# Gated-DeltaNet chunk inverses taken in pairs, the first chunk of each pair in reversed token order

## The chip, the cores and the metric

The kernel runs on one core of a Trainium2 chip. The metric is device time in microseconds (us). In profile rows PE is TensorE (its matmuls; PEld is its weight loads), DVE is VectorE, ACT is ScalarE, POOL is GpSimd and SP is SyncE.

## The reference

One step of a two-layer decoder trunk (float32, width 1024) for a prompt of 512 tokens and a sample group of 8 sequences of 4 tokens; all 544 tokens go through the same weights. Layer 0 mixes tokens with an HGRN2 recurrence, layer 1 with a gated DeltaNet; each is followed by a squared-ReLU MLP. The part that matters here is the inside of the second mixer, 8 heads of 128 by 128:

```python
G = jnp.cumsum(g, axis=-1)
decay = jnp.where(incl, jnp.exp(jnp.where(incl, diff, 0.0)), 0.0)
kk = jnp.einsum('nbhtk,nbhsk->nbhts', k, k)
M = jnp.eye(C, dtype=F32) + jnp.where(strict, beta[..., :, None] * kk * decay, 0.0)
u = lax.linalg.triangular_solve(M, v * beta[..., None], left_side=True, lower=True)
w = lax.linalg.triangular_solve(M, k * (beta * jnp.exp(G))[..., None], left_side=True, lower=True)
...
v_new = uc - jnp.einsum('bhtk,bhkv->bhtv', wc, S)
o = jnp.einsum('bhtk,bhkv->bhtv', qc, S) + jnp.einsum('bhts,bhsv->bhtv', ac, v_new)
S = glc[..., None, None] * S + jnp.einsum('bhsk,bhsv->bhkv', kc, v_new)
```

The kernel uses chunks of 128 tokens, so each head has four prompt chunks, and it needs the inverse of four unit lower triangular 128 by 128 matrices M.

## The kernel before

Everything is kept feature-major: a tile has 128 features as partitions and the 544 tokens along the row. The projections are float32 products made of three fp32r products (high by high, high by low, low by high); their matmuls all have one line, L411, and they come in steps of 6 (`tiles`, one of 8 slices of the contraction). Four units of 48 of them make one head's q, k, v and gate.

Each engine has its own program, and the order within an engine is as written; semaphores (`Steps`) join them. In the second mixer a loop runs over the heads. Its body on TensorE is `gdn_rec`, on ScalarE and VectorE `gdn_head`. While a head's recurrence runs, the three engines also prepare the next head: `gdn_prepare(slot, nxt)` is called between the steps, with the slots L0 to L6 beside the inverse and C0 to C2 beside the state update. TensorE fills its waits with projections for the coming heads: `more(2)` after the first product of a level and `more(1)` after the second (12 and 6 matmuls of L411), `later(1)` to `later(3)` in the state update. In the head before the last (head 6) `later` is empty, and in the last one (head 7) `more` is empty; there `later` does the output projection.

The inverse is built by doubling. At level m (2, 4, 8, 16, 32, 64) blocks of m by m are known on the diagonal. A level is a chain over the engines:

- **x**: for each of the four chunks, TensorE multiplies with the chunk's strict triangle `NL` (128 by 128, loaded as weights) the half of the columns of the transposed inverse `Tm` that this level needs: 64 columns (L667). ScalarE copies the result to `X` (L1173).
- **dt**: again for each chunk, `Tt` as weights and 64 columns of `X` (L700). VectorE writes the blocks that count into `Tm` with a predicated copy (L1763; step `pred{m}`).
- **tr**: TensorE transposes the four chunks of `Tm` (L449), ScalarE copies them to `Tt` (L1192; step `tt{m}`), and the next level's x waits for that.

At m = 64 the second product (L741) gives 64 rows of output and is followed by a plain copy (L1754, `pred64`), then the four chunks' state update goes one after the other: ks (L752), r (L1797), vn (L755), a ScalarE copy (L1208), dS (L758), S (L1424), with the outputs L759 and L761. Small sample products (L670, L685, L690, L692, L703, L735) run between. The last products of a head are `dSs0` (L767) and `dSs1` (L773); VectorE adds each to the sample states (L1811) and then ends the preparation of the next head.

In the head's preparation, L1614 is the silu product of k, q and v, L1694 puts the first level into `Tt`, L1682 and L1699 apply the triangle masks, L1214 copies the output. GpSimd does nothing but fill a tile with ones at the start.

Of the kernel before, what the change touches and what calls it, by code (L numbers as in the profile page):

```python
# [44 lines left out]
C_EYE, C_INCL, C_NSTR, C_IND, C_RESET, C_SEQ, C_INCLS, C_NSTRS, C_HSEL = 0, 128, 256, 384, 640, 1184, 1192, 1224, 1256  # L45
# [14 lines left out]
RS, VNS = T // 2, T // 2 + P  # L60


def shape_constants():
# [19 lines left out]
    for n, m in enumerate(LEVELS):  # L83
# [5 lines left out]
        cu[:, 1, n] = hit & (rh[:, None] == 1)  # L89
# [28 lines left out]
def build(nc, x_prompt, x_sample, state_hgrn, state_gdn, state_conv, norm_mix, norm_mlp, norm_final, hgrn_w_in,  # L118
          hgrn_lb, hgrn_out_norm, hgrn_w_out, gdn_w_in, gdn_conv_w, gdn_A_log, gdn_dt_bias, gdn_out_norm, gdn_w_out,
          mlp_w_up, mlp_w_down, const_f, const_u, y_prompt, y_sample, hgrn_p, hgrn_s, gdn_p, gdn_s, conv_p, conv_s):  # L120
    with ExitStack() as ctx:
# [3 lines left out]
        def sem(name):  # L125
            return ctx.enter_context(nc.semaphore(name))
# [52 lines left out]
        QL = hg["QL"].rearrange("p (a n) -> p a n", a=2)  # L179
        gd_vbig = [gd[n][0:TS, 0:4 * P] for n in ("Tm", "spare")]  # L180
# [42 lines left out]
        def levels(lists):  # L223
# [12 lines left out]
            gp=["x", "neg", "ls", "g", "g2", "scan", "dl"],  # L236
# [38 lines left out]
        )  # L275
        dt_ready = sem("dt_bias_ready")
# [27 lines left out]
        def blocks(ap, m):  # L304
            return ap.rearrange("p (n m) -> p n m", m=m)

# [84 lines left out]
        @block.gpsimd  # L391
        def _(pool):
            nc.gpsimd.memset(ones[:], 1.0).then_inc(ones_set, 1)


        @block.tensor
        def _(pe):
# [173 lines left out]
            def gdn_pre():  # L571
                v, s, t = st["gp"]
                pe.wait_ge(v.sem, v.after("dl", 0))
# [12 lines left out]
            def gdn_prepare(slot, h):  # L586
# [10 lines left out]
                if slot in ("L3", "L4"):  # L597
# [3 lines left out]
                    for b in range(2):  # L601
                        last = mm(rr[:, 2 + b, 0:HALF], cf[:, C_IND + g * P:C_IND + (g + 1) * P],
                                  work[:, b * HALF:(b + 1) * HALF], start=True, stop=True)
# [44 lines left out]
            def gdn_rec(h, prev, nxt, more, later):  # L648
# [7 lines left out]
                for n, m in enumerate(LEVELS[1:]):  # L656
# [31 lines left out]
                    if m == 64:  # L688
                        pe.wait_ge(s.sem, s.after("vns", h))
                        mm(rr[:, 1, 0:TS], X[0:TS, VNS:VNS + P], A[0:TS, TP:T], start=True, stop=False)  # L690
# [8 lines left out]
                    for c in range(NC):  # L699
                        last = mm(rr[:, 0, 256 + c * 64:256 + (c + 1) * 64], Tt[:, c * P:(c + 1) * P],  # L700
                                  X[:, c * 64:(c + 1) * 64], start=True, stop=True)
# [1223 lines left out]
```

## Time and profile before

| | |
|---|---|
| median of 3 runs | 1917.88 us (1913.43 to 1923.1) |
| time of the profiled execution | 1921.42 us |
| its span | 1919.6 us |
| mean granted TensorE clock | 0.94 |
| PE, PEld, DVE, ACT busy | 94%, 89%, 57%, 36% |
| POOL busy | 0.4 us, 5 instructions |

The profiled execution's time is 1.8 us more than its span. Stretches of the span: the first mixer ends near 400 us, the first MLP near 860 us, the second mixer near 1461 us, and then come output projection, second MLP and the last norm. The heads of the second mixer can be told by L773: its pairs start at 996.2, 1062.3, 1128.8, 1195.2, 1260.3, 1326.7, 1392.9 and 1460.7 us. In rows of a timeline a group's time reaches from its first start to its last end; matmuls overlap, so a group takes less of the engine than that. A float32 matmul is two MATMUL records in the trace (a transpose is one), so that four products are x8.

### The profile page before, as it was taken

Reading aid. Unit: us, or ns where it says so; the run is one execution under the profiler, and the core shown is the slowest. Engines: PE = TensorE matmul, PEld = TensorE weight load, DVE = VectorE, ACT = ScalarE, POOL = GpSimd, SP = SyncE. Lnnn points to the kernel's source line nnn. Section 1 sums busy time; section 2 is a strip of 40 time slices with the busy share of each in tenths; the row PEclk is TensorE's granted clock in tenths of the full one; section 3 lists DMA queues with packets and bytes.
Section 4 is the critical chain, followed back from the end, with each engine's and each line's share of the span. In section 5 each row is a group of like instructions: output and inputs, shape, how many; then the busy total and the mean of one; then the engine's idle time right before and its main releaser. Section 6 shows DMA issues by size and latency. Waiting matters only on the chain. (4 is left out here: it accounts for less than half of the span.)

```text
span 1919.6 us, 33969 instructions
## 1 busy us (share of the span) xinstructions
PE 1795.0 (94%) x13227; PEld 1699.2 (89%) x13227; DVE 1089.1 (57%) x1960; ACT 689.8 (36%) x1150; POOL 0.4 (0%) x5
## 2 busy tenths in 40 slices
PE   6999999989999999987899999999888999999997
PEld 5989999879999898986888888888768999999996
DVE  5777887755444343564567667766724543434344
ACT  5555555422222121223345445544512222222222
POOL 0000000000000000000000000000000000000000
PEclk9989999979999999997899999999758999999997
DMA  5222222213333232331121221122101323333321
GB/s 165 64 70 76 75 78 67 68 58 89 88 88 88 75 88 72 88 79 34 46 58 26 67 58 42 38 58 60 32 24 46 89 88 89 88 88 87 88 76 47
DMA packets 257436, 134.54 MB, mean 70 GB/s; under 512 B 6698, under 2 KB 256004, under 8 KB 257348
## 3 DMA queue, kind: packets, MB, share of 16 engines
q1 hardware_dynamic: 219488, 112.49, 20.6%
q10 hardware_dynamic: 37860, 20.76, 3.8%
q8 instruction: 69, 1.13, 0.2%
q14 instruction: 19, 0.16, 0.0%
HBM read 121.24 MB, written 12.00 MB: 69 GB/s over the span
## 5 line engine op out<-in xcount | busy, mean ns | idle before, releaser
L411 PE MATMUL pj<-xh,w_hi 128*128 128x272 f32 x2064 | 462.2, 306 | 22.2 <-DVE w_lo L1336 9.8
L867 ACT ACTIVATE w_hi<-w_raw 128x1024 fp32r<-128x1024 f32 x209 | 220.7, 1056 | 627.5 <-PE pj L411 624.9
L411 PE MATMUL pj<-xh,w_lo 128*128 128x272 f32 x2064 | 435.7, 293 | 0.0
L411 PE MATMUL pj<-xl,w_hi 128*128 128x272 f32 x2064 | 434.5, 293 | 0.0
L411 PEld LDWEIGHTS pj<-xh,w_hi 128*128 128x128 f32 x2064 | 330.8, 193 | 47.5 <-issue 25.8
L411 PEld LDWEIGHTS pj<-xl,w_hi 128*128 128x128 f32 x2064 | 332.7, 193 | 0.0
L411 PEld LDWEIGHTS pj<-xh,w_lo 128*128 128x128 f32 x2064 | 331.5, 194 | 0.0
L411 PE MATMUL pj<-oh,w_hi 128*128 128x272 f32 x1280 | 269.0, 292 | 14.3 <-DVE ol L1392 7.0
L1336 DVE TENSOR_TENSOR w_lo<-w_raw,w_hi 128x1024 fp32r<-128x1024 f32 x209 | 254.9, 1220 | 44.8 <-ACT w_hi L867 44.8
L411 PE MATMUL pj<-oh,w_lo 128*128 128x272 f32 x1280 | 266.8, 290 | 0.0
L411 PE MATMUL pj<-ol,w_hi 128*128 128x272 f32 x1280 | 265.9, 289 | 0.0
L411 PEld LDWEIGHTS pj<-oh,w_hi 128*128 128x128 f32 x1280 | 203.1, 190 | 18.0 <-DVE ol L1392 7.9
L411 PEld LDWEIGHTS pj<-ol,w_hi 128*128 128x128 f32 x1280 | 203.2, 190 | 0.0
L411 PEld LDWEIGHTS pj<-oh,w_lo 128*128 128x128 f32 x1280 | 201.8, 191 | 0.0
L1832 DVE TENSOR_TENSOR ws<-pj,rstd 128x544 f32<-128x544 f32 x64 | 46.4, 725 | 198.9 <-PE pj L411 194.5
L1844 DVE TENSOR_TENSOR xT<-xT,pj 128x544 f32<-128x544 f32 x48 | 34.6, 721 | 167.9 <-PE pj L411 167.9
L449 PE MATMUL rr<-cf,ws 128*128 128x128 f32 (+2 forms) x440 | 73.2, 305 | 13.3 <-ACT ws L1273 4.8
L449 PEld LDWEIGHTS rr<-cf,ws 128*128 128x128 f32 (+2 forms) x440 | 53.6, 153 | 25.2 <-issue 10.4
L667 PEld LDWEIGHTS rr<-ws 128*128 128x128 f32 x384 | 52.0, 208 | 21.6 <-ACT ws L1192 16.7
L1372 DVE TENSOR_TENSOR xT<-xT,pj 128x544 f32<-128x544 f32 x32 | 23.1, 721 | 81.9 <-PE pj L411 81.9
L667 PE MATMUL rr<-ws 128*128 128x64 f32 x384 | 56.9, 295 | 10.1 <-ACT ws L1192 7.8
L509 PEld LDWEIGHTS rr<-ws 128*128 128x128 f32 x448 | 59.5, 204 | 5.0 <-DVE ws L1494 3.5
(278 smaller groups left out, 2040.8 us busy)
## 6 DMA issues: line engine op xcount, KB each, us to landing
w_raw<-in_mlp_w_up_dram SPq DMA_DIRECT2D x64, 512.0 KB, 3.9
w_raw<-in_mlp_w_down_dram SPq DMA_DIRECT2D x64, 512.0 KB, 3.7
w_raw<-in_hgrn_w_in_dram SPq DMA_DIRECT2D x32, 512.0 KB, 4.0
w_raw<-in_gdn_w_in_dram SPq DMA_DIRECT2D x32, 512.0 KB, 4.2
out_dram<-S ACTq DMA_DIRECT2D x16, 512.0 KB, 3.5
S<-in_state_hgrn_dram ACTq DMA_DIRECT2D x8, 512.0 KB, 4.0
w_raw<-in_hgrn_w_out_dram SPq DMA_DIRECT2D x8, 512.0 KB, 3.6
S<-in_state_gdn_dram ACTq DMA_DIRECT2D x8, 512.0 KB, 4.0
```

Source lines behind the costliest of these rows:

```text
L411: last = mm(pj[:, s, b, 0:HALF], w[:, s, k, :], v[:, k, b * HALF:(b + 1) * HALF], start=(k == 0 and a == 0), stop=(k == KT - 1 and a == 2))
L449: return nc.tensor.transpose(out, in_, cf[0:n, C_EYE:C_EYE + n])
L509: last = mm(rr[:, n % 2, c * 64:(c + 1) * 64], KL[:, n % 2, c * P:(c + 1) * P], QL[:, n % 2, c * 64:(c + 1) * 64], start=True, stop=True)
L667: last = mm(rr[:, 0, c * 64:(c + 1) * 64], NL[:, cols], first_half(Tm[:, cols], m), start=True, stop=True)
L867: f(w_hi[:, c % SPLIT], w_raw[:, slot], ACT.Copy).then_inc(w_high, 1)
L1336: tt(w_lo[:, c % SPLIT], w_raw[:, c % RAW], w_hi[:, c % SPLIT], ALU.subtract).then_inc(w_low, 1)
L1372: tt(halves(xT[:, k]), halves(xT[:, k]), computed(U, r, k), ALU.add).then_inc(unit_out, 1)
L1832: tt(halves(B[:, k % 2]), computed(U, r, k), halves(rstd[:]), ALU.mult).then_inc(unit_out, 1)
L1844: tt(halves(xT[:, k]), halves(xT[:, k]), computed(U, g * (2 * KT), KT + k), ALU.add).then_inc(unit_out, 1)
```

## The change

The first chunk of each of the two pairs (chunks 0 and 2) is kept in reversed token order in everything that the chunk's matrices are made of. A matrix that was upper triangular becomes lower triangular by that, and so the columns that one chunk's inverse needs at a level and the rows that the other one needs lie in complementary halves. From level 4 on, one 128 by 128 weight tile holds the needed half of both chunks' `NL` (called `NLm`, put together by GpSimd in two copies a level), one holds the needed half of both chunks' `Tt` (`Ttm`, put together by ScalarE in two copies), and one product with 128 columns replaces two with 64. The transposes and level 2 stay as they were. The parts:

- TensorE: x at levels 4 to 64, dt at 4 to 32 and the product of level 64 are 2 products with 128 columns in place of 4 with 64. x of a level waits for GpSimd too.
- ScalarE: `tt2` to `tt16` are two copies of 128 elements in place of one of 512; the output copy is two of 256, one of them reversed; some copies before the first head are split in three.
- VectorE: each `pred` is two instructions of half the size, `pred64` too; silu of q, k and v is two of 256 in place of one of 512; the mask products keep their size; one step (`turn`, three copies) is new before the first head.
- GpSimd: 10 copies a head, 128 elements a partition each.
- Two products that spread a row over the partitions read 32 rows of `ones` and `work` in place of 128.

```diff
+        NLm = [gd["spare"][:, a * 2 * P:(a + 1) * 2 * P] for a in range(2)]
+        Ttm = gd["X"][:, TTM:TTM + 2 * P]
...
+        def pair_half(ap, m, odd, half):
+
+            return over_pairs(ap)[:, :, odd * P:(odd + 1) * P].rearrange("p q (n two m) -> p q n two m", two=2, m=m)[:, :, :, half, :]
...
+        def interleaved(ap, m, odd):
+
+            return ap.rearrange("p (q n two m) -> p q n two m", q=2, two=2, m=m)[:, :, :, odd]
+
+        def earlier(ap, q, m):
+
+            return bass.AP(ap.tensor, ap.offset + q * 2 * P + m, [ap.ap[0], [P - m, 2], [2 * m, P // (2 * m)], [1, m]])
...
+            def mix(h):
+
+                va, t = st["ga"][0], st["gr"][2]
+                for n, m in enumerate(LEVELS[2:], 1):
+                    waits = []
+                    if m == 4:
+                        waits.append((va.sem, fixed(pool, va.after("nl", h))))
+                        if not isinstance(h, int):
+                            waits.append((t.sem, fixed(pool, t.after("dSs1", h - 1))))
+                    if m >= 16:
+                        waits.append((t.sem, fixed(pool, t.after(f"x{m // 4}", h))))
...
+                    for odd in range(2):
+                        last = nc.gpsimd.tensor_copy(interleaved(NLm[n % 2], m, odd), pair_half(gd["NL"][:, 0:TP], m, odd, odd))
+                    mixed.did(last, f"m{m}")
...
-                    for c in range(NC):
-                        cols = slice(c * P, (c + 1) * P)
-                        last = mm(rr[:, 0, c * 64:(c + 1) * 64], NL[:, cols], first_half(Tm[:, cols], m),
-                                  start=True, stop=True)
...
+                        pe.wait_ge(mixed.sem, mixed.after(f"m{m}", h))
+                        for q in range(NC // 2):
+                            last = mm(rr[:, 0, q * P:(q + 1) * P], NLm[n % 2][:, q * P:(q + 1) * P], earlier(Tm, q, m),
+                                      start=True, stop=True)
...
+                        for q in range(NC // 2):
+                            last = mm(rr[:, 0, 256 + q * P:256 + (q + 1) * P], Ttm[:, q * P:(q + 1) * P],
+                                      X[:, q * P:(q + 1) * P], start=True, stop=True)
...
-                for c in range(NC):
-                    last = mm(rr[0:m, 0, 256 + c * m:256 + (c + 1) * m], X[:, c * m:(c + 1) * m],
-                              Tt[:, c * P + m:(c + 1) * P], start=True, stop=True)
+                for q in range(NC // 2):
+                    last = mm(rr[:, 0, 256 + q * P:256 + (q + 1) * P], X[:, q * P:(q + 1) * P], later_ends(Tt, q),
+                              start=True, stop=True)
...
-                    last = f(Tt[:, 0:TP], rr[:, 1, :], ACT.Copy)
+                    if m < LEVELS[-2]:
+                        for odd in range(2):
+                            last = f(interleaved(Ttm, 2 * m, odd), pair_half(rr[:, 1, :], 2 * m, odd, odd), ACT.Copy)
+                    else:
+                        last = f(Tt[:, 0:TP], rr[:, 1, :], ACT.Copy)
...
-                s.did(f(oo[:, 0:TP], rr[:, 1, :], ACT.Copy), "oo")
+                f(blocks(oo[:, 0:TP], P)[:, 0::2, ::-1], blocks(rr[:, 1, :], P)[:, 0::2, :], ACT.Copy)
+                s.did(f(blocks(oo[:, 0:TP], P)[:, 1::2, :], blocks(rr[:, 1, :], P)[:, 1::2, :], ACT.Copy), "oo")
...
-                    tt(dst[:, 0:TP], pr[:, row, 0:TP], ng[:, row, 0:TP], ALU.mult)
+                    for (o, a), (_, b) in list(zip(by_position(dst, pr[:, row, 0:T]), by_position(dst, ng[:, row, 0:T])))[0:2]:
+                        tt(o, a, b, ALU.mult)
...
-                    last = pred(first_half(Tm[:, 0:TP], m), blocks(mask[:, 1, n, 0:TP // 2], m), blocks(rr[:, 0, 256:512], m))
+                    for odd in range(2):
+                        last = pred(pair_half(Tm[:, 0:TP], m, odd, 1 - odd), pair_cols(mask[:, 1, n, 0:TP // 2], m, odd),
+                                    pair_cols(rr[:, 0, 256:512], m, odd))
```

TensorE's program in the last head, before, from x of level 4 to x of level 32 (one row is a group of equal matmuls; L667 is x, L700 dt, L449 a transpose, L685 the sample states):

```order
L667 MATMUL rr<-ws 128x64 x4
L700 MATMUL rr<-ws 128x64 x4
L449 MATMUL rr<-cf,ws 128x128 x8
L449 MATMUL rr<-cf,ws 32x128
L667 MATMUL rr<-ws 128x64 x4
L685 MATMUL rr<-ws,S 128x4 x8
L700 MATMUL rr<-ws 128x64 x4
L449 MATMUL rr<-cf,ws 128x128 x4
L667 MATMUL rr<-ws 128x64 x4
L700 MATMUL rr<-ws 128x64 x4
```

And the same place after (L726 is x, L764 dt, L502 a transpose, L744 the sample states):

```order
L726 MATMUL rr<-ws 128x128 x2
L764 MATMUL rr<-ws 128x128 x2
L502 MATMUL rr<-cf,ws 128x128 x8
L502 MATMUL rr<-cf,ws 32x128
L726 MATMUL rr<-ws 128x128 x2
L744 MATMUL rr<-ws,S 128x4 x8
L764 MATMUL rr<-ws 128x128 x2
L502 MATMUL rr<-cf,ws 128x128 x4
L726 MATMUL rr<-ws 128x128 x2
L764 MATMUL rr<-ws 128x128 x2
```

Only the number and the width of the x and dt products differ; nothing changes its place.

VectorE's program in the loop over the heads, before, up to `pred8` (L1606 and L1427 are the next head's convolution, L1749 a small sample step, L1763 the predicated copy):

```order
L1606 SCALAR_TENSOR_TENSOR pr<-xp,hcw,pr 128x568
L1293 REGISTER_ALU
L1427 SCALAR_TENSOR_TENSOR ng<-pr 128x568
L1293 REGISTER_ALU
L1749 TENSOR_TENSOR rt<-rr,eGs 128x32
L115 REGISTER_ALU
L1763 COPY_PREDICATED ws<-cu,rr 128x32x8
```

And after (L1687 and L1505 are the convolution, L1835 the sample step, L1852 the predicated copy):

```order
L1687 SCALAR_TENSOR_TENSOR pr<-xp,hcw,pr 128x568
L1371 REGISTER_ALU
L1505 SCALAR_TENSOR_TENSOR ng<-pr 128x568
L1371 REGISTER_ALU
L1835 TENSOR_TENSOR rt<-rr,eGs 128x32
L116 REGISTER_ALU
L1852 COPY_PREDICATED ws<-cu,rr 128x2x8x8 x2
```

Nothing moved here either: the predicated copy has become two, at the same place behind the next head's convolution.

## Rows read from the trace of the kernel before

**Rows 1.** The page, its first two parts: span and busy time

```profile
span 1919.6 us, 33969 instructions
PE 1795.0 (94%) x13227; PEld 1699.2 (89%) x13227; DVE 1089.1 (57%) x1960; ACT 689.8 (36%) x1150; POOL 0.4 (0%) x5
```

**Rows 2.** Busy by stretch: length, PE, PEld, DVE, ACT, POOL, PEclk, DMA share, GB/s

```profile
1195.00:1260.00 65.00, 60.87 (x451) 54.01 (x450) 45.20 (x102) 31.89 (x70) 0.00 (x0) 1.00 0.19 51
1260.00:1326.00 66.00, 61.91 (x449) 55.05 (x447) 44.91 (x102) 31.96 (x70) 0.00 (x0) 0.97 0.18 50
1278.50:1289.70 11.20, 11.06 (x88) 10.43 (x88) 10.67 (x19) 5.46 (x13) 0.00 (x0) 1.00 0.14 41
1291.00:1298.00 7.00, 6.12 (x45) 5.39 (x44) 5.09 (x12) 6.92 (x16) 0.00 (x0) 1.00 0.13 31
1396.00:1447.40 51.40, 43.74 (x187) 38.91 (x188) 12.46 (x34) 8.71 (x21) 0.00 (x0) 0.50 0.08 22
```

**Rows 3.** PE timeline: the last product (`dSs1`) of heads 3, 4 and 5

```profile
1195.17 0.67 PE L773 MATMUL rr<-ws,kdTs 32*128 32x512 f32 x1
1260.30 0.67 PE L773 MATMUL rr<-ws,kdTs 32*128 32x512 f32 x1
1326.70 0.67 PE L773 MATMUL rr<-ws,kdTs 32*128 32x512 f32 x1
```

**Rows 4.** PE timeline of head 5: start, time, line, count, idle before

```profile
1266.25 0.49 PE L411 MATMUL pj<-xh,w_hi 128*128 128x272 f32 x2 [0.48 <-DVE xp L1597]
1271.45 1.10 PE L667 MATMUL rr<-ws 128*128 128x64 f32 x8 [0.17 <-ACT ws L1194]
1275.64 1.10 PE L700 MATMUL rr<-ws 128*128 128x64 f32 x8 [1.10 <-ACT ws L1173]
1291.67 1.10 PE L667 MATMUL rr<-ws 128*128 128x64 f32 x8 [0.58 <-ACT ws L1192]
1311.44 0.38 PE L755 MATMUL rr<-ws 128*128 128x128 f32 x2
1313.26 1.06 PE L622 MATMUL rr<-ws 128*128 128x128 f32 x8
```

**Rows 5.** DVE timeline of head 5

```profile
1278.58 0.76 DVE L1738 TENSOR_TENSOR ws<-rr,gcols 128x256 f32<-128x256 f32 x2 [1.29 <-PE rr L449]
1280.98 2.50 DVE L1606 SCALAR_TENSOR_TENSOR pr<-xp,hcw,pr 128x568 f32<-128x568 f32 x3
1284.28 0.43 DVE L1763 COPY_PREDICATED ws<-cu,rr 128x256 f32<-128x256 uint8 x1
1289.83 0.45 DVE L1763 COPY_PREDICATED ws<-cu,rr 128x256 f32<-128x256 uint8 x1 [0.16 <-PE rr L700]
1303.10 0.69 DVE L1614 TENSOR_TENSOR ws<-pr,ng 128x512 f32<-128x512 f32 x1
1308.77 0.29 DVE L1421 COPY Sp<-rr 128x128 f32<-128x128 f32 x1 [0.75 <-PE rr L758]
```

**Rows 6.** ACT timeline of head 5

```profile
1291.02 0.60 ACT L1192 ACTIVATE ws<-rr 128x512 f32<-128x512 f32 x1 [2.20 <-PE rr L449]
1297.41 0.60 ACT L1192 ACTIVATE ws<-rr 128x512 f32<-128x512 f32 x1
1316.67 0.28 ACT L1208 ACTIVATE ws<-rr 128x128 f32<-128x128 f32 x1 [4.24 <-PE rr L755]
```

**Rows 7.** PE timeline of head 7

```profile
1424.89 1.97 PE L700 MATMUL rr<-ws 128*128 128x64 f32 x8 [0.47 <-ACT ws L1173]
1427.45 1.12 PE L449 MATMUL rr<-cf,ws 128*128 128x128 f32 x4 [0.59 <-DVE ws L1763]
1429.25 1.97 PE L667 MATMUL rr<-ws 128*128 128x64 f32 x8 [0.47 <-ACT ws L1192]
```

**Rows 8.** PE timeline ahead of the first head, and POOL's instructions

```profile
865.57 1.30 PE L449 MATMUL rr<-cf,gt 128*128 128x128 f32 x5 [10.72 <-ACT gt L1031]
L393 POOL MEMSET ones<- 128x128 f32 x1 | 0.2, 204 | 0.3 <-POOLq L1913 0.3
```

More of the change, by code:

```diff
@@ L393, in _ @@
             nc.gpsimd.memset(ones[:], 1.0).then_inc(ones_set, 1)
+            def mix(h):
[8 more added lines that the diff above has]
+                        waits.append((t.sem, fixed(pool, t.after(f"x{m // 4}", h))))
+                    pool.wait_ge(c_in, 16 * N_CONST)
+                    for sem_, value in waits:
+                        pool.wait_ge(sem_, value)
+                    for odd in range(2):
+                        last = nc.gpsimd.tensor_copy(interleaved(NLm[n % 2], m, odd), pair_half(gd["NL"][:, 0:TP], m, odd, odd))
+                    mixed.did(last, f"m{m}")
+            mix(0)
+            with pool.Fori(1, H) as h:
+                mix(h)
         @block.tensor
@@ L572, in gdn_pre @@
                 v, s, t = st["gp"]
-                pe.wait_ge(v.sem, v.after("dl", 0))
+                pe.wait_ge(v.sem, v.after("turn", 0))
                 pe.wait_ge(s.sem, s.after("eg", 0))
@@ L601, in gdn_prepare @@
                     for b in range(2):
-                        last = mm(rr[:, 2 + b, 0:HALF], cf[:, C_IND + g * P:C_IND + (g + 1) * P],
-                                  work[:, b * HALF:(b + 1) * HALF], start=True, stop=True)
+                        last = mm(rr[:, 2 + b, 0:HALF], ones[32 * g:32 * (g + 1), :],
+                                  work[32 * g:32 * (g + 1), b * HALF:(b + 1) * HALF], start=True, stop=True)
                     t.did(last, name)
@@ L664, in gdn_rec @@
                         pe.wait_ge(s.sem, s.after(f"tt{LEVELS[n]}", h))
-                    for c in range(NC):
-                        cols = slice(c * P, (c + 1) * P)
-                        last = mm(rr[:, 0, c * 64:(c + 1) * 64], NL[:, cols], first_half(Tm[:, cols], m),
-                                  start=True, stop=True)
+                    if n == 0:
+                        for c in range(NC):
+                            cols = slice(c * P, (c + 1) * P)
+                            half = Tm[:, cols].rearrange("p (n two m) -> p n two m", two=2, m=m)[:, :, 1 - c % 2, :]
+                            last = mm(rr[:, 0, c * 64:(c + 1) * 64], NL[:, cols], half, start=True, stop=True)
+                    else:
[3 more added lines that the diff above has]
+                                      start=True, stop=True)
                     if smp:
@@ L698, in gdn_rec @@
                     pe.wait_ge(s.sem, s.after(f"x{m}", h))
-                    for c in range(NC):
-                        last = mm(rr[:, 0, 256 + c * 64:256 + (c + 1) * 64], Tt[:, c * P:(c + 1) * P],
-                                  X[:, c * 64:(c + 1) * 64], start=True, stop=True)
+                    if n == 0:
+                        for c in range(NC):
+                            last = mm(rr[:, 0, 256 + c * 64:256 + (c + 1) * 64], Tt[:, c * P:(c + 1) * P],
+                                      X[:, c * 64:(c + 1) * 64], start=True, stop=True)
+                    else:
+                        for q in range(NC // 2):
+                            last = mm(rr[:, 0, 256 + q * P:256 + (q + 1) * P], Ttm[:, q * P:(q + 1) * P],
+                                      X[:, q * P:(q + 1) * P], start=True, stop=True)
                     if smp:
```

79 lines of the change are left out of this document (54 added, 25 removed).

## The prediction

> **What bounds the kernel now.** I read the page first [rows 1]: TensorE is busy for 94% of the span, VectorE for 57%. That looks like a kernel in which every matmul taken away counts. So the next view is the busy time by stretch in the second mixer [rows 2]. A head takes 65 to 66.5 us, TensorE is busy for about 61 of it and VectorE for 45. A busy share does not say who waits for whom, so I then read the timelines of the three engines in head 5, one of the five heads of the loop, in order of time. There TensorE waits seldom, but each wait is for a copy of ScalarE or a product of VectorE [rows 4], and two stretches have no slack on another engine: from 1278.58 to 1289.7 VectorE is busy for 10.67 of 11.20 us, and from 1291.0 to 1298.0 ScalarE for 6.92 of 7.00 us [rows 2]. In both, the step of the inverse that TensorE needs next (the predicated copies of levels 8 and 16, the copy `tt32`) is queued behind work for the next head [rows 5, 6]. TensorE's fill work just covers them. The loop heads are balanced: TensorE is as late as VectorE and ScalarE, not later.
>
> The last head is another case. There is no next head and no fill, its clock is 1.2 GHz (granted 0.50 over 51.4 us, rows 2), and TensorE waits only for the step that it has itself just released, 0.47 to 0.59 us each [rows 7]. There every matmul in the chain counts.
>
> **What one product costs.** Eight records with 128 columns (L622, four products) take 1.06 us and two (L755) take 0.38: (1.06 - 0.38) / 6 = 0.11 us a record at 2.4 GHz. Eight records with 64 columns (L667) take 1.10 us, as much as eight with 128 [rows 4]. So a product costs the same with twice the columns, and a group that falls from 8 records to 4 gives back 4 x 0.11 = 0.45 us. At 1.2 GHz the step is (1.97 - 1.12) / 4 = 0.21 us [rows 7], and a group gives back 0.85 us. Nine groups a head are of this kind (x of 4 to 64, dt of 4 to 32); the product of level 64 loads only 64 columns of weights before, and I take 0.2 us for it. That removes 9 x 0.45 + 0.2 = 4.25 us of TensorE's work from each of heads 0 to 6, and 9 x 0.85 + 0.25 = 7.9 us from head 7.
>
> **What the other engines get.** ScalarE: one copy of 512 elements is 0.60 us, one of 128 is 0.28 [rows 6]; if the second starts 0.1 us before the first ends, two take 0.46, so `tt2` to `tt16` come 0.14 us earlier. VectorE: a predicated copy of 256 elements is 0.43 to 0.45 us, a plain copy of 128 is 0.29 [rows 5]; two halves should be 0.48, 0.05 more. Silu is 0.69 for 512 elements [rows 5]; two halves are some 0.09 more, three times a head. The output copy grows by 0.1 us in front of transposes that have 12 matmuls of fill ahead of them: nothing. Reversed rows are not in the trace; bounds are nothing and a doubling of 0.35 us per half, and I take nothing, as VectorE's strided products of 256 elements are no slower.
>
> **A loop head, step by step** (head 5, its own times):
> - Level 4: x waits 0.17 us for `tt2` [rows 4] and starts 0.14 earlier; it is 0.45 shorter, but the transposes behind it wait for VectorE, so 0.35 is left. The wait of 1.10 us before dt is for ScalarE, which is busy for the next head behind those transposes: it stays. dt gives 0.45; VectorE, still in L1336, gives the predicated copy only part of it. When the key transposes are done, 0.55 us is gained.
> - From there VectorE has no gap (L1738 at 1278.58) until `pred16`, except the 0.16 us in front of it [rows 5]. x and dt of levels 8 and 16 are 1.8 us shorter, and all of this turns into waits of TensorE for `pred8` and `pred16`. Gained: 0.55 + 0.16 - 2 x 0.05 = 0.6.
> - `tt16` 0.14 earlier: x of level 32, which waits 0.58 us for it [rows 4], starts 0.75 earlier. Then ScalarE has no gap up to `tt32` at 1297.41 [rows 6], so x of level 64 is also 0.75 earlier, and the 0.9 us of x and dt of level 32 is lost.
> - x of level 64 gives 0.45: 1.2. Level 64's product, then silu and `pred64` in VectorE's gapless row take back 0.15, and silu of v about 0.05: **1.0 us a head** of 4.25.
>
> **The sum.** Heads 1 to 5: 5 x 1.0 = 5.0. Head 0 has no head before it to finish, so VectorE has three full rows less (about 0.7 us each, as silu); of the 1.8 us lost in that stretch I count half or so: 2.0. Head 6 has the same front and no projections behind: 1.2. Head 7: 7.9, plus two `tt` copies on the path 0.3, less the split copies 0.3: 7.9. Before the first head TensorE stands 10.72 us for a chain of small steps that ends in a 0.65 us exponential [rows 8]; the split copies and the new step put perhaps 0.2 on it, and silu in the first preparation 0.3: -0.5. GpSimd: 10 copies a head of 128 elements; the only row of its size is a fill, 0.204 us [rows 8]. Level 64's may start when x of level 16 is done, and from x of level 32 at 1291.67 [rows 4] to the end of `tt32` at 1298.0 [rows 6] alone are 6.3 us, so TensorE won't wait for them. What they cost is what they take from VectorE: nothing, or 8 of 10 copies at full length in heads 0 to 6, 56 x 0.2 = 11.4 us. No row shows the two together; I take 0.3 us a head, nearer to nothing as the copies are short against the convolution they meet (three in 2.50 us, rows 5): -2.1. Together 5.0 + 2.0 + 1.2 + 7.9 - 0.5 - 2.1 = **13.5 us**. The profiled execution's 1921.4 us would become 1907.9; that execution is 3.5 us above the median, and from the median 1917.9 I forecast **1904.4 us**.
>
> **The rivals.**
> - *TensorE bounds all heads after all*, since it is busy for 94%: then 7 x 4.25 + 7.9 - 0.5 = 37 us, 1881. Against it stand the two gapless stretches. Chance 0.1.
> - *GpSimd holds VectorE* (the case on the other side). Place: level 32's copies start behind x of level 8, in the middle of VectorE's gapless stretch, those of level 64 behind x of 16, those of 4 and 8 behind `dSs1`, where TensorE waits 0.48 us for VectorE [rows 4]. Without the GpSimd term the gain is 15.6 us. With 0.204 us for each of 56 copies it is 4.2 (1913.7); at 0.28 us a copy it is gone; from 0.45 us a copy the kernel is slower by more than 0.5%. At 0.5 us: 56 x 0.5 - 15.6 = 12.4 us slower, 1930. Chance of about no change by this 0.15, of slower 0.1. The Trainium skill bears on it: GPSIMD Engine Reference, section Key points, says that GpSimd shares its SBUF interfaces with VectorE and contends with instructions in a two-port mode or with two SBUF inputs. The convolution in that stretch has two SBUF inputs, so by this rule the sum would lie nearer to the 4.2 us; no row here shows it.
> - *The clock.* Head 4, at full clock throughout, takes 65.13 us and head 5, with granted 0.97, takes 66.40 [rows 2, 3]: one dip costs 1.27 us. TensorE will wait some 3 us more in each head. Two more dips in each of seven heads would cost 17.8 us: 1922. Against it: the added waits lie where TensorE has slack then, so a dip there costs less. Chance of ending near no change 0.12. The other way, the last head's stretch of 51.4 us at 1.2 GHz, with 43.7 us of TensorE in it, could get a higher clock as its waits get shorter against its work; half of that back would be about 11 us more, 1893. Chance 0.05. The Trainium skill (TensorE: Matmul & The Clock Gate, Part 1) says that the granted clock follows how busy TensorE has been of late; the last head's 0.50 agrees.
> - *The change doesn't do what it says*: if 128 columns cost twice 64, nothing would be gained. The row of L622 excludes it.
>
> **How the numbers follow.** Forecast 0.48, own range 1898 to 1911. A measurement of this kernel tells about 0.5%, 9.6 us, from no change, so faster means below 1908.3: most of the forecast (0.40), TensorE-bound 0.1 and the better clock 0.05 make 0.55; same 0.35; slower 0.10. Leaving out the TensorE-bound case (0.1) and the slower one (0.1) gives 1886 to 1919.
>
> **What the profile after would show.** In the loop heads: x and dt of levels 4 to 64 as x4 in 0.6 us; TensorE's waits grow by about 3 us a head, with new ones of some 1 us in front of the transposes of levels 8 and 16, for the predicated copy; the period of L773 falls by about 1 us; VectorE's stretch between kdT and `pred16` keeps its 11 us. In the last head: from dt of level 16 to x of level 32 it is 4.36 us before [rows 7] and should be about 3.4; all of its chain shrinks by 8. POOL: 80 copies. Wrong would be: L1606 longer than 0.83 us each (2.50 for three) where a POOL copy runs, POOL copies over 0.4 us, a period that falls by 4 us, or a granted clock in heads 1 to 5 below 0.95.

## The result

The changed kernel takes **1900.27 us** (median of 7 runs, 1897.56 to 1903.4) where the kernel before takes 1917.88 (7 runs); the ratio is 0.9907, with a 95% interval of 0.9896 to 0.9918. That is 17.6 us less; the forecast was 13.5 less (1904.4), with a stated range of 1898 to 1911. The profiled execution has a span of 1898.5 us against 1919.6, so 21.1 us less. Of these, 4.2 us lie ahead of the second mixer's first convolution step (at 889.15 us before, at 884.94 after), where nothing was changed; over the 14 profiled executions of this document that point lies between 878.6 and 889.1 us.

The page of the kernel after, its span and busy time, and the row of GpSimd's copies:

```profile
span 1898.5 us, 33650 instructions
PE 1762.5 (93%) x12907; PEld 1658.5 (87%) x12907; DVE 1095.6 (58%) x2043; ACT 684.4 (36%) x1194; POOL 43.2 (2%) x85
L441 POOL COPY ws<-ws 128x128 f32<-128x128 f32 x80 | 42.8, 568 | 1360.9 <-DVE ws L1766 914.1
```

Busy time by stretch after: head 4, head 5, VectorE's row from the key decay to `pred16` in head 5, and the last head; columns as in [rows 2]:

```profile
1183.00:1248.20 65.20, 59.25 (x413) 51.57 (x412) 46.10 (x111) 31.20 (x75) 5.26 (x10) 0.97 0.19 50
1248.20:1312.50 64.30, 57.84 (x412) 49.95 (x412) 46.09 (x111) 31.22 (x75) 5.26 (x10) 1.00 0.18 51
1266.20:1277.30 11.10, 9.92 (x75) 9.09 (x76) 10.71 (x20) 5.17 (x13) 2.83 (x4) 1.00 0.15 43
1378.10:1437.90 59.80, 50.68 (x250) 42.46 (x250) 17.21 (x49) 10.89 (x33) 4.47 (x10) 0.63 0.07 19
```

VectorE's row ahead of `pred16` is as long and as full as before (10.71 of 11.10 us; 10.67 of 11.20 in [rows 2]), while TensorE's busy time in it fell from 11.06 to 9.92. A head at full clock has 3.0 us less of TensorE's work than before (57.84 against 60.87, [rows 2]) and is 0.8 us shorter (64.33 against 65.13, [rows 3]).

TensorE's timeline of head 5 after, the places that [rows 4] shows of before and the new waits (L726 is x, L764 dt, L502 the transposes, L485 the feature sum):

```profile
1259.50 0.71 PE L726 MATMUL rr<-ws 128*128 128x128 f32 x4
1263.59 0.71 PE L764 MATMUL rr<-ws 128*128 128x128 f32 x4 [1.10 <-ACT ws L1246]
1272.58 0.66 PE L502 MATMUL rr<-cf,ws 128*128 128x128 f32 x4 [1.13 <-DVE ws L1852]
1277.88 0.66 PE L502 MATMUL rr<-cf,ws 128*128 128x128 f32 x4 [0.19 <-DVE ws L1852]
1279.15 0.71 PE L726 MATMUL rr<-ws 128*128 128x128 f32 x4 [0.50 <-ACT vTs L1277]
1294.52 1.18 PE L485 MATMUL rr<-ws,ones 128*128 128x272 f32 x4 [0.42 <-DVE ws L1705]
```

Eight records became four, and the group behind dt of level 4 starts 0.46 us after it (1263.59 to 1264.05) where it was 0.92 (1275.64 to 1276.56). The copy of x of level 4 is waited for as long as before (1.10 us). In front of the transposes of level 8 there is a new wait of 1.13 us for the predicated copy. VectorE in the same head, against [rows 5]:

```profile
1266.22 0.76 DVE L1824 TENSOR_TENSOR ws<-rr,gcols 128x256 f32<-128x256 f32 x2 [1.29 <-PE rr L502]
1272.04 0.49 DVE L1852 COPY_PREDICATED ws<-cu,rr 128x128 f32<-128x128 uint8 x2
1277.34 0.48 DVE L1852 COPY_PREDICATED ws<-cu,rr 128x128 f32<-128x128 uint8 x2
1278.66 0.74 DVE L1696 TENSOR_TENSOR ws<-pr,ng 128x256 f32<-128x256 f32 x2
```

And TensorE in the last head, against [rows 7]:

```profile
1404.45 1.22 PE L764 MATMUL rr<-ws 128*128 128x128 f32 x4 [0.47 <-ACT ws L1246]
1406.33 1.11 PE L502 MATMUL rr<-cf,ws 128*128 128x128 f32 x4 [0.65 <-DVE ws L1852]
1407.97 1.23 PE L726 MATMUL rr<-ws 128*128 128x128 f32 x4 [0.32 <-ACT ws L1267]
```

From dt of level 16 to x of level 32 it is 3.52 us where it was 4.36.

**A table for all that follows.** Length of the heads in the profiled executions, from one head's last product (`dSs1`) to the next head's. In brackets: how many short stretches of 3.4 us at 1.2 GHz begin in a loop head. A head without one has a granted clock of 1.00, with one 0.97, with two 0.95. A ratio is taken against runs of the kernel before that were made beside that kernel (medians 1916.1 for e1 to e4, 1919.8 for e5 to e7, 1917.7 for e8 to e11, 1917.4 for e12), so ratios compare better than medians do.

| kernel | median us | ratio (95%) | heads 1 to 5 | head 6 | head 7 |
|---|---|---|---|---|---|
| before | 1917.9 | 1 | 66.1 (1), 66.4 (1), 66.4 (1), 65.1 (0), 66.4 (1) | 66.2 | 67.8 |
| after | 1900.3 | 0.9907 (0.9896 to 0.9918) | 64.7 (2), 65.1 (1), 65.1 (1), 65.2 (1), 64.3 (0) | 65.5 | 59.9 |
| e1 | 1934.3 | 1.0091 (1.0075 to 1.0107) | 67.9 (2), 68.2 (2), 68.2 (2), 68.2 (2), 68.2 (2) | 66.6 | 62.3 |
| e2 | 1932.8 | 1.0091 (1.0076 to 1.0106) | 67.9 (2), 68.2 (2), 68.2 (2), 68.2 (2), 68.2 (2) | 66.4 | 69.3 |
| e3 | 1910.3 | 0.9966 (0.9952 to 0.998) | 64.7 (1), 65.0 (2), 65.1 (2), 65.1 (2), 65.1 (1) | 65.6 | 69.3 |
| e4 | 1902.9 | 0.9926 (0.9912 to 0.994) | 64.8 (2), 65.1 (1), 64.5 (0), 65.1 (2), 65.1 (1) | 64.9 | 59.9 |
| e5 | 1926.7 | 1.0041 (1.0026 to 1.0057) | 67.4 (1), 68.2 (2), 67.6 (1), 66.2 (0), 67.7 (1) | 64.1 | 68.9 |
| e6 | 1900.8 | 0.9908 (0.9892 to 0.9924) | 64.7 (1), 65.0 (1), 64.4 (0), 65.0 (1), 65.0 (1) | 65.8 | 59.9 |
| e7 | 1914.6 | 0.9983 (0.997 to 0.9995) | 66.1 (1), 65.2 (0), 65.1 (0), 65.1 (0), 66.4 (1) | 63.8 | 68.7 |
| e8 | 1934.5 | 1.0095 (1.0081 to 1.011) | 69.6 (3), 67.0 (1), 68.3 (2), 68.3 (2), 68.3 (2) | 66.4 | 67.4 |
| e9 | 1913.4 | 0.9975 (0.9964 to 0.9986) | 65.5 (1), 65.9 (1), 65.9 (1), 66.6 (2), 67.7 (3) | 64.0 | 62.0 |
| e10 | 1913.4 | 0.9975 (0.996 to 0.999) | 65.2 (1), 65.9 (1), 67.0 (2), 68.0 (3), 65.5 (1) | 62.5 | 59.9 |
| e11 | 1906.5 | 0.9947 (0.9932 to 0.9963) | 65.7 (2), 64.5 (1), 63.8 (0), 66.0 (2), 63.8 (0) | 65.3 | 61.8 |
| e12 | 1893.6 | 0.9873 (0.9852 to 0.9895) | 63.1 (0), 63.4 (0), 64.0 (1), 63.4 (0), 64.1 (1) | 62.6 | 62.2 |

### The profile page after: what moved, and what is told of

The parts are those of the page before. It is cut to its first block and busy times, and to the rows that moved or that the text cites. A ratio compares the mean times of both kernels' runs of the same rounds, so it can differ in the third digit from the quotient of the medians.

```text
span 1898.5 us, 33650 instructions
## 1 busy us (share of the span) xinstructions
PE 1762.5 (93%) x12907; PEld 1658.5 (87%) x12907; DVE 1095.6 (58%) x2043; ACT 684.4 (36%) x1194; POOL 43.2 (2%) x85
## 3 DMA queue, kind: packets, MB, share of 16 engines
q1 hardware_dynamic: 219488, 112.49, 21.1%
q8 instruction: 68, 1.11, 0.2%
## 5 line engine op out<-in xcount | busy, mean ns | idle before, releaser
L502 PE MATMUL rr<-cf,ws 128*128 128x128 f32 (+2 forms) x440 | 74.6, 310 | 20.8 <-DVE ws L1852 9.6
L502 PEld LDWEIGHTS rr<-cf,ws 128*128 128x128 f32 (+2 forms) x440 | 54.4, 154 | 36.8 <-DVE ws L1852 14.4
L441 POOL COPY ws<-ws 128x128 f32<-128x128 f32 x80 | 42.8, 568 | 1360.9 <-DVE ws L1766 914.1
L562 PEld LDWEIGHTS rr<-ws 128*128 128x128 f32 x448 | 58.7, 202 | 5.0 <-DVE ws L1572 3.5
```

The source lines that it names most:

```text
L441: last = nc.gpsimd.tensor_copy(interleaved(NLm[n % 2], m, odd), pair_half(gd["NL"][:, 0:TP], m, odd, odd))
L502: return nc.tensor.transpose(out, in_, cf[0:n, C_EYE:C_EYE + n])
L562: last = mm(rr[:, n % 2, c * 64:(c + 1) * 64], KL[:, n % 2, c * P:(c + 1) * P], QL[:, n % 2, c * 64:(c + 1) * 64], start=True, stop=True)
```

## The experiments

**e1, e2, e3: the pairs in the last head alone, nowhere, in the loop heads alone.** The token order and all that belongs to it stays; the products go chunk by chunk where `paired` is false:

```
+                    elif not paired:      # e1: nxt is None; e2: never; e3: nxt is not None
+                        for c in range(NC):
+                            cols = slice(c * P, (c + 1) * P)
+                            half = Tm[:, cols].rearrange("p (n two m) -> p n two m", two=2, m=m)[:, :, 1 - c % 2, :]
+                            last = mm(rr[:, 0, c * 64:(c + 1) * 64], NL[:, cols], half, start=True, stop=True)
+                    else:
```

(dt and the `tt` copy likewise; GpSimd mixes only for paired heads.)

> The new token order stays in all heads; the products of x (levels 4 to 64) and dt (levels 4 to 32) are paired only in head 7, heads 0 to 6 take eight records again, with one tt copy each and no GpSimd copies. Theory (loop heads are bound by VectorE and ScalarE, the last head by TensorE): the last head gives 7.9 us, the order itself costs about 2, so 1912 us against 1917.9 before. Rival (the loop heads give nothing, what the changed kernel gained there is the clock's doing): the same 17.6 us as the fully changed kernel, about 1900.

> Token order, split predicated copies, split silu and the merged dt of level 64 stay; no other product is paired, one tt copy a level, GpSimd copies nothing. Theory: overhead alone, 0.5 us ahead of the first head, about 0.25 a loop head (silu 0.09 three times, predicated copies 0.05 each in a gapless row of VectorE), less 0.4 for level 64's dt in the last head: 2 us slower, 1920. Rival (reversed rows or split instructions cost more than the forecast, and the pairs gain more than it): 5 us slower or more, 1923 and up. Rival (order is free): 1918.

> Pairs in heads 0 to 6 only, with their GpSimd copies; head 7 takes eight records. Theory: all of the gain but the last head's 7.9 us, so about 9.7 us faster, 1908; heads 0 to 6 then gave 11 to 12 us over the order alone, 1.3 to 1.6 each. Rival (loop heads give nothing): 1918 to 1920.

The order without pairs is 16.7 us slower than before (1932.8 against 1916.1), not 2, and e1, expected at 1912, takes 1934.3; e3 came at 1910.3 where 1908 was expected. The pairs in the loop heads then give 22.5 us (e3 against e2), 3.1 us a head in the traces; those in the last head give 10.0 us in the medians (after against e3; 11.3 by the ratios) and 9.4 in the traces. e1 and e2 have the same ratio although e1's last head is 7.0 us shorter in its trace. In e1's profiled execution 3.9 us more than in e2's lie ahead of the first convolution step and 4.9 behind the last head, with a wait of 2.79 us for weights of the second MLP that the other traces don't have; where the timed runs lose the 7 us was not seen.

Where did the order's 17 us come from? Head 5 of e2 in pieces, the 1.2 GHz stretches apart:

```profile
1261.30:1282.50 21.20, 19.32 (x144) 16.87 (x143) 12.35 (x38) 8.02 (x23) 0.00 (x0) 1.00 0.36 104
1282.80:1286.20 3.40, 3.40 (x19) 3.40 (x17) 2.52 (x5) 1.44 (x4) 0.00 (x0) 0.52 0.00 0
1286.50:1306.40 19.90, 18.97 (x136) 16.42 (x136) 15.10 (x34) 11.55 (x25) 0.00 (x0) 1.00 0.09 26
1306.70:1310.10 3.40, 3.40 (x18) 3.11 (x17) 3.35 (x8) 1.98 (x4) 0.00 (x0) 0.52 0.00 0
1310.50:1329.50 19.00, 17.71 (x132) 15.76 (x130) 11.57 (x28) 8.54 (x17) 0.00 (x0) 1.00 0.11 30
```

Two short stretches at half clock, and all five heads of e2 have them at the same two places, 21 and 45 us behind `dSs1`. Before, one head has one or none. In e2 both places lie at the end of a group of 8 products of 4 columns (16 records; the expectations call them 16 products): from 0.2 us before the end of its last record to 1.0 us behind it, and 0.2 to 1.7 us behind it in the kernel before. That these groups let the clock fall was a theory to test.

**e5, e6, e7: those groups widened**, in the order-only kernel, after and before.

```
-    last = mm(rr[:, 1, b * SLEN:(b + 1) * SLEN], S0[:, b, :], K[:, TP + b * SLEN:TP + (b + 1) * SLEN], start=True, stop=True)
+    last = mm(rr[:, 1, b * SLEN:TS], S0[:, b, :], K[:, TP + b * SLEN:T], start=True, stop=True)
```

(the products with `qe` likewise; those add up, so in these three kernels the sample rows of the output differ)

> The order-only kernel (e2) with one more edit: the two groups of 16 products with 4 columns a head (sample states, named sks and os) take all columns up to the end of the sample block, 32 down to 4; those of os then add wrong values in the sample rows, so the output differs there. Theory formed after e1 to e4: the order itself costs nothing; its 17 us are TensorE's clock. In the traces each half-clock stretch of 3.4 us in heads 1 to 5 begins 0.4 to 2 us behind one of these two groups; the order-only kernel has two in each head (68.2 us), the one before has one (66.4) or none (65.1). If the groups are what lets the clock fall, the stretches go, the heads take 65.1 us, and the kernel about 1910 (23 us less than e2's 1933). Rival (split and reversed instructions are what costs 17 us): heads stay at 68 us, 1933. Rival (something else lets the clock fall): the stretches stay where they are.

> The changed kernel with the same widening of the sks and os products (sample rows differ). Its heads take 65.1 us with one or with two half-clock stretches and 64.3 to 64.5 with none. Theory: the stretches go from the heads, 0.7 us each for six heads, some 4 us less: 1896. Rival (the last head also gets a higher clock): up to 10 us less, 1890. Rival (no effect on the clock): 1900.

> The kernel before with the same widening (sample rows differ). Theory: heads at 65.1 us throughout where most take 66.4, so 5 to 8 us less: 1908 to 1912; at an equal clock the changed kernel's heads are then 0.7 us shorter, which is the value of the pairs in a loop head without the clock. Rival (no effect on the clock): 1916.

The theory holds in part. e5 has 5 short stretches in heads 1 to 5 instead of 10 and gives back 6 us in the medians (9.6 by the ratios), of 23; e7 has 2 instead of 4, and its ratio is 0.9983; e6 changes nothing in the time. Expected were 1910, 1896 and 1908 to 1912; the medians are 1926.7, 1900.8 and 1914.6. Some of the stretches that are left begin elsewhere (34 us behind `dSs1` in e5). What lets the clock fall is therefore not settled. But these runs give heads at full clock in three kernels, to be compared without the clock. The first row is e7 (the work of before), the second e5 (the order alone), the third e6 (the work of after):

```profile
1186.60:1251.70 65.10, 61.01 (x452) 54.15 (x452) 45.34 (x101) 31.91 (x70) 0.00 (x0) 1.00 0.19 51
```

```profile
1193.90:1260.10 66.20, 61.50 (x448) 54.02 (x448) 45.77 (x111) 31.96 (x71) 0.00 (x0) 1.00 0.18 50
```

```profile
1118.80:1183.20 64.40, 57.91 (x413) 50.04 (x412) 46.13 (x111) 31.21 (x75) 5.26 (x10) 1.00 0.19 51
```

From `dSs1` to `dSs1` the order costs 1.05 us a head (66.18 against 65.13) and the pairs give 1.85 (to after's 64.33; e6's own head is 64.37): **0.80 us a head net**, where the prediction had 1.0. Set side by side step by step, e5 loses 0.23 us up to the end of the broadcast `gb` (0.09 in front of it, 0.14 in it), 0.34 at `bb`, some 0.2 at predicated copies, and 0.25 late in the head, in VectorE's row: `pred64` in two copies (0.51 us from first start to the next instruction, 0.34 before) and silu in two halves (0.67 against 0.60).

**e8: the broadcast alone, in the kernel before.** The change also altered the products that spread a head's gate and beta over all rows. The prediction had passed over this edit.

```
-    last = mm(rr[:, 2 + b, 0:HALF], cf[:, C_IND + g * P:C_IND + (g + 1) * P],
-              work[:, b * HALF:(b + 1) * HALF], start=True, stop=True)
+    last = mm(rr[:, 2 + b, 0:HALF], ones[32 * g:32 * (g + 1), :],
+              work[32 * g:32 * (g + 1), b * HALF:(b + 1) * HALF], start=True, stop=True)
```

> The kernel before with one edit of the change alone: the broadcasts gb and bb take 32 rows of ones and of the gates in place of 128 rows of an indicator (L602). At full clock in both, the two groups and what stands behind them took 0.23 and 0.43 us more in the order-only kernel than in the one before. Theory (those two groups of four products are 0.6 us of the 1.1 us by which a loop head got longer through the new order): heads at full clock 65.13 to 65.6 or 65.7 us, some 3 to 5 us in all, unless the clock's stretches fall otherwise: 1920 to 1922 against 1917. Rival (the order of the tokens, the split instructions, cost it all): 65.13 stays.

e8's heads 2 and 3, with one and with two short stretches:

```profile
1062.60:1129.60 67.00, 62.88 (x453) 55.40 (x452) 45.18 (x101) 31.98 (x70) 0.00 (x0) 0.97 0.18 49
1129.60:1197.90 68.30, 64.20 (x453) 56.92 (x452) 45.18 (x101) 32.08 (x70) 0.00 (x0) 0.95 0.18 48
```

With one short stretch the head takes 66.98 us where it takes 66.41 before: 0.57 us for this edit, as expected. Group by group, against before's head 5, whose stretch lies at the same place: 0.23 us up to the end of `gb`, 0.34 at `bb`, nothing behind. TensorE in e8's head 2, the second group (`bb`) and what follows it, and the same place in head 5 of before:

```profile
1095.29 1.18 PE L602 MATMUL rr<-ws,ones 32*128 32x272 f32 x4
1096.40 0.52 PE L411 MATMUL pj<-xh,w_hi 128*128 128x272 f32 x2
```

```profile
1292.62 1.14 PE L602 MATMUL rr<-ws,cf 128*128 128x272 f32 x4
1293.39 0.61 PE L411 MATMUL pj<-xh,w_hi 128*128 128x272 f32 x2
```

The same four records with 32 rows in place of 128 hold the next group back by 1.11 us, not 0.77. But the median rose by 16.8 us, and the expectation of 3 to 5 was wrong: 0.57 us in seven heads are 4. Most of the rest goes with the clock. In the traces heads 1 to 5 are 10.9 us longer than before: 2.9 are the edit, and the other 8 go with six more short stretches (10 against 4), 1.3 us each. In the timed runs the mean granted clock has a median of 0.935 in e8 against 0.943 before; over 68 runs of the kernel before, 0.001 of clock goes with 1.4 us (a line fitted through them), so 0.008 is 11 us by this estimate. The line holds for one kernel only: e5 takes 12 us more than e7 at the same mean clock (0.945). e2 (0.938) and e8 have the same pattern, a head of 68.2 to 68.3 us with two short stretches each at the same places.

**e4: three times the GpSimd copies.**

```
+    for again in ("a", "b", ""):     # each level's two copies three times, each behind the one before
         for odd in range(2):
             last = nc.gpsimd.tensor_copy(interleaved(NLm[n % 2], m, odd), pair_half(gd["NL"][:, 0:TP], m, odd, odd))
```

> The changed kernel with every GpSimd copy made three times over (30 a head instead of 10, 160 more in all, the same values to the same place). Theory (where GpSimd meets VectorE, GpSimd's copy is what gets longer, 0.29 to 0.9 us, and VectorE's convolution keeps its 0.81 us a step): no change, 1900 within 2 us, though POOL is busy for some 130 us. Rival (GpSimd takes its own time from VectorE, 0.2 us a copy, 140 more copies in heads 0 to 6): 28 us slower if all count, 10 to 15 if those in the gapless stretches do: 1910 or more.

POOL is busy for 112.9 us instead of 43.2, and the time is 1902.9 where 1898 to 1902 was expected. The ratio is 0.9926 (0.9912 to 0.994) against the changed kernel's 0.9907 (0.9896 to 0.9918): the intervals just overlap, so a small cost, 3.6 us by the ratios for 160 more copies, is not excluded, but the 28 us of the rival are, and so are its 10 to 15. A head at full clock by busy time, and VectorE's convolution in the groups of instructions:

```profile
1121.60:1186.10 64.50, 57.85 (x412) 49.95 (x412) 46.42 (x111) 31.20 (x75) 14.17 (x30) 1.00 0.19 51
```

```profile
L1692 DVE SCALAR_TENSOR_TENSOR pr<-xp,hcw,pr 128x568 f32<-128x568 f32 x72 | 58.4, 811 | 6.2 <-ACT pr L1124 4.5
```

Twenty more copies a head cost VectorE 0.3 us of busy time (46.42 against 46.09), its convolution 2 ns a step (811 against 809). A head at full clock is 0.2 us longer (64.51 against 64.33). What gets longer is GpSimd's copy: two of them take 1.67 us beside the loop head's convolution and 0.53 us in the last head, where VectorE is mostly idle (POOL's timeline after):

```profile
1337.89 1.67 POOL L441 COPY ws<-ws 128x128 f32<-128x128 f32 x2 [6.17 <-PE rr L726]
1404.11 0.53 POOL L441 COPY ws<-ws 128x128 f32<-128x128 f32 x2 [4.36 <-PE rr L726]
```

**e9, e10, e11: which engine sets a loop head.** Steps of VectorE, in e11 of ScalarE too, are moved in the changed kernel: e9 puts `pred8` ahead of the third tap of k's convolution, e10 also puts the third tap of q behind `pred16`, e11 also puts the z unit's weight split behind the copy of x of level 4 (ScalarE) and behind `pred4` (VectorE).

```
     for j in taps:
+        if j == 3 and between is not None:
+            between()                                  # e9: sr1 and pred8
...
-    convolve("q", "qtap", 1, Q_ROW)                    # in L3
+    convolve("q", "qtap", 1, Q_ROW, (1, 2))            # e10: in L3
+    convolve("q", "qtap", 1, Q_ROW, (3,))              # e10: in L4, behind pred16
...
     s.did(last, f"x{m}")
+    if nxt is not None and m == 4:
+        high(nxt * 4, U_GIN + 3)                       # e11: no longer in L1
```

> The changed kernel with the predicated copies of level 8 moved on VectorE ahead of the third tap of k's convolution; nothing else. TensorE's wait in front of the transposes of level 8 (1.13 us in head 5) goes. Theory of the prediction (VectorE has no gap from the key decay to pred16, so it sets when level 16 goes on): the wait in front of level 16's transposes grows from 0.19 to about 1.2 us, the period stays at 65.1 (one half-clock stretch) and the kernel at 1900. Rival (TensorE sets the time of the stretch): 1.1 us a head in seven heads, 1892 to 1893.

> As e9, and the third tap and the minimum of q's convolution (1.6 us of VectorE) moved behind pred16. Theory: VectorE's gapless row ahead of pred16 is 1.6 us shorter, so what e9 could not give comes: 0.8 to 1.2 us a head, period 64 us, 1893 to 1895. Rival (ScalarE's gapless row up to tt32 or the later silu takes it back): 1899 to 1901. Rival (TensorE-bound, e9 gave it already): the same as e9.

> As e10, and the weight split of the z unit put behind the copy of x of level 4 on ScalarE and behind pred4 on VectorE, where TensorE waits 1.10 us for that copy (head 5) in both kernels. Theory: another 0.5 to 1 us a head, 1888 to 1890. Rival (the unit's weights then come late for TensorE's fill, or VectorE's row behind is pushed by 1.2 us): as e10 or up to 5 us slower.

Expected were 1900, 1893 to 1895 and 1888 to 1890; the medians are 1913.4, 1913.4 and 1906.5. e9 loses 0.8 us a head at one short stretch (65.9 against 65.1), and its kernel 13 us: some 6 are those 0.8 us in seven heads, its last head is 2.1 us longer, and two of its heads have two and three short stretches. The timelines of VectorE, ScalarE and TensorE in e9's head 2:

```profile
1082.41 0.49 DVE L1841 COPY_PREDICATED ws<-cu,rr 128x128 f32<-128x128 uint8 x2 [0.31 <-PE rr L764]
1085.85 0.75 DVE L1509 SCALAR_TENSOR_TENSOR ng<-pr,ng 128x568 f32<-128x568 f32 x1 [0.49 <-ACT ng L1126]
```

```profile
1084.43 0.68 ACT L1124 ACTIVATE ng<-ng 128x568 f32<-128x568 f32 x1 [0.56 <-DVE ng L1505]
1085.72 0.43 ACT L1267 ACTIVATE ws<-rr 128x128 f32<-128x128 f32 x2
```

```profile
1086.28 0.71 PE L726 MATMUL rr<-ws 128*128 128x128 f32 x4 [1.55 <-ACT ws L1267]
1090.25 0.66 PE L502 MATMUL rr<-cf,ws 128*128 128x128 f32 x4 [0.56 <-DVE ws L1868]
```

The wait in front of the transposes is gone, and TensorE stands 1.55 us one step later: the copy `tt8` is queued on ScalarE behind exp and log of k, which need the convolution that is now later. VectorE's row got two gaps, 0.31 and 0.49 us, and `pred16` came 0.77 us later. So it is not TensorE that sets this stretch (taking its wait away gave nothing, as it came back one step later), and a gap in VectorE's row costs its full length, as the prediction had it; but ScalarE stands right behind VectorE, which it had not. e10 shows the same 1.56 us wait for `tt8` and no gain over e9. e11 alone brings something: its wait in front of dt of level 4 fell from 1.10 to 0.15 us, and its heads at full clock take 63.8 us, 0.5 less than after's 64.3; yet its median is 6 us above the changed kernel's, with two short stretches in heads 1 and 4 and a last head of 61.8 us.

**e12: 128 rows again, and the x4 copy first.** The broadcast reads one indicator column for all 128 columns; of e11 only the z unit's weight split is kept.

```
-    last = mm(rr[:, 2 + b, 0:HALF], ones[32 * g:32 * (g + 1), :],
-              work[32 * g:32 * (g + 1), b * HALF:(b + 1) * HALF], start=True, stop=True)
+    last = mm(rr[:, 2 + b, 0:HALF], cf[:, C_ROW[g]:C_ROW[g] + 1].broadcast_to([P, P]),
+              work[:, b * HALF:(b + 1) * HALF], start=True, stop=True)
```

> The changed kernel with two edits: the broadcasts gb and bb take 128 rows again (an indicator column that is read for all 128 columns), and the weight split of the z unit stands behind the copy of x of level 4 on ScalarE and behind pred4 on VectorE. Theory: gb and what follows gets 0.14 us shorter and bb 0.34, the wait of 1.10 us in front of dt of level 4 goes; a loop head at full clock takes 63.6 to 64.0 us where the changed kernel takes 64.33, 3 to 6 us in all: 1895. Rival (VectorE's and ScalarE's gapless rows take back the 128-row part): 63.8, as e11. Rival (a new rhythm brings more half-clock stretches, as in e9 to e11): 1900 to 1906, with heads at full clock no longer than 64.

Head 4 of e12 by busy time, and dt of level 4 (its wait was 1.10 us) and the broadcast `bb` in TensorE's timeline there:

```profile
1175.60:1239.00 63.40, 57.17 (x413) 50.02 (x412) 46.01 (x111) 31.21 (x75) 4.79 (x10) 1.00 0.19 52
```

```profile
1190.05 0.71 PE L766 MATMUL rr<-ws 128*128 128x128 f32 x4 [0.16 <-ACT ws L1249]
1206.12 1.08 PE L657 MATMUL rr<-ws,cf 128*128 128x272 f32 x4
```

This is the fastest kernel, 1893.6 us, ratio 0.9873, and its interval (0.9852 to 0.9895) lies below the changed kernel's. A head at full clock takes 63.4 us, 0.9 less than after and 0.4 less than e11, and three of five heads are at full clock. Its two edits were not made one by one, so how the 0.9 us divide between them is open.

## Why the prediction was right, point by point

- **The time.** 17.6 us against 13.5 forecast, inside the stated range. By the profiled executions: heads 1 to 5 gave 6.1 us (330.5 to 324.4; forecast 5.0), of which 4.0 are the five heads at full clock and 2.1 come from short stretches that cost less after than before, head 6 0.65 (1.2), head 7 7.87 (7.9), and the stretch from the first convolution step to the end of head 0 3.9 (1.5), with a granted clock of 0.90 against 0.87 there, which carries part of it. GpSimd took little (forecast 2.1): by e4, whose 20 more copies lengthen a full-clock head by 0.2 us, 10 copies are 0.1 us a head, an estimate. Together 18.5; 4.2 lie ahead of the change, and 1.6 were lost behind it, where TensorE is at half clock for 31.5 us in place of 27.1. That the sum fits within 4 us is partly luck: the loop heads at full clock gave less than forecast, and the clock and the stretch before head 1 more.
- **The price of a product** held: x and dt of eight records became four, and the group behind starts 0.41 to 0.46 us sooner (forecast 0.45). By busy time it is less: a group's row falls from 1.10 to 0.71 us, and a head has 3.6 us less (e5 against e6), not 4.25; TensorE's idle time in a head at full clock grew by 2.3 us, not 3. And e2 against e1, both at half clock through the inverse, is 7.0 us for the last head (forecast 7.9 net).
- **Head by head.** At full clock the gain is 0.80 us, not 1.0. Along the head (after's head 5 against e7's head at 1186.6): key transposes 0.32 us earlier (forecast 0.55), transposes behind `pred16` 0.39 (0.6), x of level 32 0.43 (0.75), x of level 64 0.59 (0.75), dt of level 64 1.13 (1.2), end 0.80 (1.0). The shape is right: little until `pred16`, next to nothing between there and x of level 64, most from level 64. The 1.2 us that TensorE has gained by the end of level 8's dt are down to 0.1 at the transposes behind it, in a new wait of 1.13 us, as forecast; the one at level 16 is 0.19 instead of about 1.
- **The step that was missed** is an edit without a term: the broadcast with 32 rows, which the sum put at nothing without a reason. It costs 0.57 us a head in the kernel before. In the changed kernel it lies partly in time that TensorE would wait anyhow; there it was only taken out together with e11's move.
- **VectorE sets the loop heads**: half right. The gapless row stayed (10.71 of 11.10 us), and e9 shows that a gap in it is paid in full. But e9 and e10 show ScalarE as late as VectorE at `tt8`, which the prediction named only for `tt32`.
- **Small terms**: two `tt` copies 0.45 us (0.46), predicated copies 0.48 to 0.50 (0.48), silu 0.07 more (0.09), the wait before the first head 10.90 after 10.72 (0.2 more), reversed rows nothing that shows: right.
- **The GpSimd rival** is out by e4 with its price of 0.2 us a copy. One sign that the prediction named for it did appear, POOL copies over 0.4 us: the 80 copies take 0.57 us in the mean and 1.72 at the longest. None of the others did: the convolution kept 0.81 us a step, the period fell by 0.8 us at full clock and not by 4, and heads 1 to 5 together have a granted clock of 0.97. So the length of a copy says nothing here of what it costs. By the Trainium skill (GPSIMD Engine Reference, section Key points) GpSimd contends with VectorE's instructions that have two SBUF inputs, as the convolution has; the trace agrees that they meet (0.53 us for two copies alone, 1.67 beside it), but here VectorE's convolution kept 809 ns a step, and GpSimd's copy paid.
- **The last head** has the right sum by luck: 7.0 us are the pairs, 2.4 come from a higher clock (e1 to after: 3.3 us at granted 0.94 in the middle, rows below, and an earlier return to full clock; a small part of the 11 us of the prediction's better-clock case), and 1.6 go the other way (e2's last head is longer than that of before, 69.3 against 67.8, by more time at half clock).

  The middle of the last head after, and the same place in e1:

```profile
1398.50:1401.80 3.30, 2.54 (x20) 2.27 (x19) 2.38 (x7) 0.93 (x2) 1.25 (x2) 0.94 0.00 0
```

```profile
1416.00:1424.00 8.00, 7.35 (x35) 6.94 (x33) 3.04 (x8) 1.37 (x4) 1.60 (x2) 0.50 0.00 0
```

- **The clock rival** was judged by its price (one short stretch 1.27 us), and in the changed kernel it did not come (5 short stretches in heads 1 to 5, 4 before). In e2 and e8 it did, and that is a thing the prediction gave too little weight: the kernel before pays 1.3 us for the first stretch in a head (65.1, 66.4), e8 1.3 for the second (67.0, 68.3), the order alone 1.4 and 0.6 (66.2, 67.6, 68.2), the changed kernel 0.7 for the first and nothing for the second (64.4, 65.1, 65.1), perhaps because its TensorE has waits to lose, which was not tested. With two stretches in a head the pairs are worth 3.1 us (e2 against e3); without any, 1.85. So a part of what the change gains in these runs is that its heads are insensitive to the clock. How the 17.6 us divide between that and the rest is not settled.

## What to carry to other kernels

List every edit of a diff that touches the engine with the most work and give each a number, also those that look like tidying: here one that freed constants cost 0.57 us a head. Where three engines are balanced, halving the products returned half of the TensorE time that it freed (1.85 us of 3.6, e5 against e6), and moving one step only moved the wait; look for the engine that stands second before moving anything. And compare kernels at the same granted clock, stretch by stretch, before reading a difference of a per cent as the edit's own.

## What the runs showed of the hardware

- A product with 32 rows of weights and of moving data is not cheaper than one with 128 rows of the same 272 columns: in e8 four records hold the queue for 1.11 us, against 0.97 and 0.77 in the kernel before and 0.92 and 0.72 in e12. It is not the tile (four records with 128 rows of `ones` as weights, L432, hold it for 0.91 in the kernel before) and not the row that the operands start at (`gb` reads from row 0, `bb` from row 32, and both take 1.11 in e8).
- A GpSimd copy of 128 elements takes 0.29 us when VectorE is idle (0.53 for two) and up to 0.9 beside its convolution, while VectorE loses 2 ns of 811.
- A work increase of 0.57 us in a head of 66.4 us went with a granted clock of 0.935 in place of 0.943 over the whole kernel, and with 17 us. Short stretches at 1.2 GHz came at the same two places of each head in those kernels. Widening the products of 4 columns ahead of them took away half of them in two kernels and did not change the time in the third; their cause is open.
